# Moving weight splits, an exp table, four stores and a normalisation in a decoder layer

## The reference

```python
x = x + 0.5 * swiglu(rms_norm(x, g_ffn1), w1_ffn1, w3_ffn1, w2_ffn1)      # width 2816
z = rms_norm(x, g_mix) @ w_in + b_in                                      # q | k | v | u | v_gate
attn_out, k_state, v_state = attend(q, k, v)         # window of 128, softmax with a sink per head
vg = layer_norm(gelu(vg), gm_ln_g, gm_ln_b)
gm_out = gelu(u) * chunk_spatial_mix(vg, gm_w_s, gm_b_s)
x = x + concat([attn_out, gm_out]) @ w_out + b_out
x = x + 0.5 * swiglu(rms_norm(x, g_ffn2), w1_ffn2, w3_ffn2, w2_ffn2)
x = x + sigmoid(rms_norm(x, g_ple) @ w_ple_gate) * (ple @ w_ple_proj)
y = rms_norm(x, g_final)
```

## Time and profile before

| | us |
|---|---|
| median of 3 runs | 942.0 |
| lowest, highest | 941.59, 943.26 |
| the profiled execution | 943.26 |
| its span in the trace | 941.5 |
| TensorE busy | 927.4 (98%) |
| VectorE busy | 747.5 (79%) |
| ScalarE busy | 584.9 (62%) |
| GpSimd busy | 231.4 (25%) |

### The profile page before, as it was taken

The page is one execution under the profiler, slowest core; times in us unless marked ns, Lnnn a source line. Parts: engine busy times, 40 slices in busy tenths (PEclk is TensorE's granted clock), DMA queues, the critical chain, the costliest instruction groups (busy, mean ns, idle before and its releaser), DMA issues.

```text
span 941.5 us, 19772 instructions
## 1 busy us (share of the span) xinstructions
PE 927.4 (98%) x7702; PEld 915.2 (97%) x7702; DVE 747.5 (79%) x1293; ACT 584.9 (62%) x973; POOL 231.4 (25%) x181
## 2 busy tenths in 40 slices
PE   7999999999999999999999999999999999999997
PEld 7999999999999999989999999999999999999897
DVE  6979977888888686667866588987788888869586
ACT  7748746666667574756544566775676676657343
POOL 0212222223222220000319412222222322222221
PEclk9999999999999999999999999999999999999999
DMA  8958888778887789221133798877777887778702
GB/s 249 179 102 169 152 170 160 143 141 160 170 160 140 136 162 219 69 68 46 52 96 91 140 174 162 171 151 151 164 148 133 174 171 137 160 165 172 142 24 92
DMA packets 253385, 133.42 MB, mean 142 GB/s; under 512 B 15594, under 2 KB 249412, under 8 KB 253276
## 3 DMA queue, kind: packets, MB, share of 16 engines
q1 hardware_dynamic: 177820, 93.55, 36.0%
q0 software_dynamic: 75136, 37.76, 32.4%
q10 hardware_dynamic: 336, 0.84, 0.3%
HBM read 129.57 MB, written 3.59 MB: 141 GB/s over the span
## 4 chain that ended last, share of the span: by engine, by line
PE 54%; issue 28%; POOL 9%; DMA 4%; DVE 3%; ACT 2%; SPq 1%; POOLq 0%; DVEq 0%; ACTq 0%
PE ps L2079 30%; PE ps L1990 18%; POOL w_lo L1264 4%; POOL w_lo L1272 4%; PE ps L2421 2%; PE ps L2024 1%; DMA w_lo<-in_w_in_dram 1%; PE ps L2108 1%; DMA w_lo<-in_w_ffn_dram 1%; DMA w_lo<-in_w_ple_gate_dram 1%; DMA x_rows<-in_x_prompt_dram 1%; PE ps L2297 1%; POOL w_lo L1236 1%; PE ps L2326 1%; DMA w_raw<-in_w_ffn_dram 1%
## 5 line engine op out<-in xcount | busy, mean ns | idle before, releaser
L2079 PE MATMUL ps<-xo_hi,w_lo 128*128 128x260 f32 x1008 | 284.8, 283 | 0.0
L2079 PE MATMUL ps<-xo_hi,w_hi 128*128 128x260 f32 x1008 | 284.4, 282 | 0.0
L2079 PE MATMUL ps<-xo_lo,w_hi 128*128 128x260 f32 x864 | 244.3, 283 | 0.0
L2079 PEld LDWEIGHTS ps<-xo_hi,w_hi 128*128 128x128 f32 x1008 | 189.9, 188 | 0.0
L2079 PEld LDWEIGHTS ps<-xo_hi,w_lo 128*128 128x128 f32 x1008 | 189.9, 188 | 0.0
L1500 DVE TENSOR_TENSOR w_lo<-w_raw,w_hi 128x512 fp32r<-128x512 f32 (+1 forms) x180 | 174.4, 983 | 14.3 <-ACT w_hi L941 7.2
L2079 PEld LDWEIGHTS ps<-xo_lo,w_hi 128*128 128x128 f32 x864 | 162.7, 188 | 0.0
L2079 PE MATMUL ps<-hop_hi,w_hi 128*128 128x260 f32 x560 | 158.6, 283 | 0.6 <-ACT snap L972 0.5
L2079 PE MATMUL ps<-hop_hi,w_lo 128*128 128x260 f32 x560 | 158.4, 283 | 0.0
L2079 PE MATMUL ps<-hop_lo,w_hi 128*128 128x260 f32 x560 | 158.1, 282 | 0.0
L1264 POOL DMA_DIRECT2D w_lo<-in_w_ffn_dram x60 | 76.8, 1279 | 276.4 <-ACT w_lo L948 276.4
(11 more groups left out here) (320 smaller groups left out, 2058.8 us busy)
## 6 DMA issues: line engine op xcount, KB each, us to landing
w_raw<-in_w_ffn_dram SPq DMA_DIRECT2D x88, 256.0 KB, 4.4
w_lo<-in_w_ffn_dram POOLq DMA_DIRECT2D x88, 256.0 KB, 5.5
w_a<-in_w_ffn_dram SPq DMA_DIRECT2D x36, 512.0 KB, 5.8
w_raw<-in_w_ffn_dram SPq DMA_DIRECT2D x20, 512.0 KB, 5.9
w_a<-in_w_ffn_dram SPq DMA_DIRECT2D x32, 192.0 KB, 4.0
w_raw<-in_w_ffn_dram SPq DMA_DIRECT2D x32, 192.0 KB, 4.1
w_lo<-in_w_ffn_dram POOLq DMA_DIRECT2D x32, 192.0 KB, 5.1
w_raw<-in_w_in_dram SPq DMA_DIRECT2D x10, 512.0 KB, 4.7
```

The source lines that it names most:

```text
L2079: ins = pe.matmul(ps[:, b, 0:Q], w[:, cc, k * P:(k + 1) * P], m_, start=(first and k == 0 and t == 0), stop=(k == kn - 1 and t == 2), skip ...
```

## The change

- In `ffn_steps()` the steps `("hi","next",3)` and `("hi","next",4)` go. In the first stage their splits move into the mixer, to steps (1,2) and (2,2), by a wider condition in ACT's and POOL's loops. In the second stage ACT and POOL do keys 3, 4 and 5 of the last stage (gates 1, 2, 3) right behind `ffn_stage(1)`, where key 5 stood alone.
- Tables: units 3, 5 and 7 of the mixer move from DVE's subtraction to `summed`; gates 1, 2 and 3 move from `summed` to POOL's subtraction. DVE's remaining subtractions for units 4 and 13 come at other steps.
- `stat_spread` and `evac` 0 and 1 move from step (2,1) to (2,0).
- The five `norm` steps move from (11,7) to (12,0); `norm_rsqrt` stays.
- The exp on one column is removed.
- The four window stores are issued by ACT behind the copies of `kv_turn`, behind a wait for them, no longer by SP.

```diff
@@ ffn_steps
-                steps += [("lo", "next", 2), ("hi", "next", 3), ("hi", "next", 4)]
+                steps.append(("lo", "next", 2))
@@ mixer_steps
-        (2, 1): [("stat_spread",), ("evac", 0), ("evac", 1)],
+        (2, 0): [("stat_spread",), ("evac", 0), ("evac", 1)],
-        (11, 7): [("s_take",), ("norm_rsqrt",), ("norm", 3), ("norm", 4), ("norm", 0), ("norm", 1), ("norm", 2)],
+        (11, 7): [("s_take",), ("norm_rsqrt",)],
+        (12, 0): [("norm", 3), ("norm", 4), ("norm", 0), ("norm", 1), ("norm", 2)],
@@ hybrid_decoder_layer
-        summed = [("up", 0, n) for n in range(4, N_STD)] + last_keys(0)[:2]
-        summed += [("up", 1, n) for n in range(3, N_STD)] + last_keys(1)[:2] + last_keys(1)[3:6]
-        first_out = [("in", u) for u in range(3, 8)] + [("in", u) for u in range(8, N_IN)] + [("out", m) for m in range(3)]
-        low_steps = [("gemm", 1, 6), ("gemm", 1, 7), ("gemm", 3, 7), ("gemm", 4, 7), ("gemm", 5, 7)] + [("gemm", u - 2, 7) for u in range(8, N_IN)] + [("gemm", 12, 7), ("gemm", 13, 2), ("out", 0, 4)]
+        summed = [("up", 0, n) for n in range(4, N_STD)] + last_keys(0)[:2] + last_keys(0)[3:8:2]
+        summed += [("up", 1, n) for n in range(3, N_STD)] + last_keys(1)[:2]
+        first_out = [("in", 4), ("in", 6)] + [("in", u) for u in range(8, N_IN)] + [("out", m) for m in range(3)]
+        low_steps = [("gemm", 2, 7), ("gemm", 4, 7)] + [("gemm", u - 2, 7) for u in range(8, N_IN - 1)] + [("gemm", 12, 0), ("gemm", 12, 7), ("gemm", 13, 2), ("out", 0, 4)]
@@ sync
-            def store_windows():
-                ... (four dma_start)
-                elif u == 8:
-                    store_windows()
@@ scalar and gpsimd, loop over the mixer's steps
-                if kind == "gemm" and arg[1] == (2 if arg[0] < 6 else 5) and 2 < arg[0] < 13:
+                if kind == "gemm" and arg[1] == (2 if arg[0] < 6 else 5) and 0 < arg[0] < 13:
@@ scalar
-                elif kind == "scores" and arg[0] == 0:
-                    nc.scalar.activation(s_st[:, 6:7], ones[0:64, 0:1], ACT.Exp)
                     nc.scalar.activation(k_rows[0:TS, 1, :], ps[0:TS, 7, 2 * P:3 * P], ACT.Copy).then_inc(kv_taken, 1)
+                    act.wait_ge(kv_taken, 4)
+                    act.dma_start(o["v_win_prompt"]...)
+                    ... (the other three, as they were on SP)
@@ scalar and gpsimd, behind ffn_stage(1)
-            split_hi(last_keys(1)[5])
+            for key in last_keys(1)[3:6]:
+                split_hi(key)
```

More of the change, by code:

```diff
@@ L1117, in _ @@
                     nc.scalar.activation(k_rows[0:TS, 1, :], ps[0:TS, 7, 2 * P:3 * P], ACT.Copy).then_inc(kv_taken, 1)
+                    act.wait_ge(kv_taken, 4)
+                    act.dma_start(o["v_win_prompt"][0, 0].rearrange("w h d -> w (h d)"), v_rows[:, NB - 1, :]
+                                  ).then_inc(out_done, 16)
+                    act.dma_start(o["k_win_prompt"][0, 0].rearrange("w h d -> w (h d)"), k_rows[:, 0, :]
+                                  ).then_inc(out_done, 16)
+                    act.dma_start(o["v_win_sample"][0, :, W - 1].rearrange("b h d -> b (h d)"), v_rows[0:TS, NB, :]
+                                  ).then_inc(out_done, 16)
+                    act.dma_start(o["k_win_sample"][0, :, W - 1].rearrange("b h d -> b (h d)"), k_rows[0:TS, 1, :]
+                                  ).then_inc(out_done, 16)
                 elif kind == "soft":
@@ L1319, in _ @@
             ffn_stage(1)
-            split_lo(last_keys(1)[5])
+            for key in last_keys(1)[3:6]:
+                split_lo(key)
             clear_ssq(4)
```

## The result

The changed kernel takes 949.9 us (median of 4 runs, 948.41 to 950.1) against 942.38 us for the kernel before beside it: the ratio is 1.0077, with a 95% interval of 1.0058 to 1.0094. It is 7.5 us slower. I had forecast 944.6 in a range up to 947.4: the direction was right, the size too small, and the time lies outside the range. Run again beside three other kernels it took 949.94 us against 941.39, a ratio of 1.0093 (1.0078 to 1.0108). A ratio in this text is estimated from all runs of the two kernels, not divided out of the medians; the two can differ by up to 0.13%.

What follows compares the result with a forecast made beforehand. PE, busy 98% of the span, was taken as the bound. From the profiled 943.26 us, -2.1 - 1.6 + 1.1 + 1.7 + 1.9 + 0.3 = +1.3 gave 944.5, from the median 944.9; forecast 944.6, range 941.2 to 947.4.

Steps and rivals of the forecast that it cites:

- Part 1: Last stage's gates 1 to 3 by GpSimd's subtraction: DMA wait -2.1, low-clock stretch -1.6, VectorE's held add +1.1 us.
- Part 2: First softmax: exp's table load and four store issues on ACT start the first exp 3.07 us later; PE stalls +1.7.
- Part 3: Mixer units 3, 5 and 7 summed by DMA: unit 3's lands 10.2 us after issue, +1.9 us; units 5 and 7 cost 0.
- rival B: At unit 3 the copies hold the DMA: 4.8 us instead of 1.9, plus low clock; 948.4 at most; chance 0.12.
- bound of 4.8: Upper case for PE's wait at unit 3: 3.3 us of delay added to 8.2, plus 1.6 of spread.
- bound of 3.5: Upper bound of PE's wait at unit 3 if its DMA lands 11.8 us behind issue.
- The clock: Rival: any new wait of 1.7 or 1.9 us brings a low-clock stretch there, +1.6 us, 946.2; chance 0.16.
- Part 4: Norms at (12,0) end at about 462.6, +0.3 us, from -0.1 to +0.9; spread at (2,0) 0, up to +0.3.

Runs made afterwards that it cites:

- experiment 1: The changed kernel with unit 3 of the mixer back on VectorE's subtraction: 945.91 us, ratio 1.0041 to the kernel before.
- experiment 3: The kernel before with the one-column exp removed (941.85 us), the four window stores moved to ACT (941.34 us), or both (943.48 us).
- experiment 2: The changed kernel with the two 508 KB window copies issued behind the load of the mixer's last unit: 944.45 us, ratio 1.003.

## Why the prediction was wrong

- **Part 1 held.** The DMA wait of 2.1 and the stretch behind it went, and the add held by GpSimd cost 0.95 where I had 1.1. The kernel with the gates alone and the one with the wait show both halves. The forecast's -2.1, -1.6 and +1.1 are -2.1, -1.6 and +0.95 in the profiles. By the medians the gates alone won 1.8 us, not 2.75; it would fit if only some executions of the kernel before have the stretch, which isn't shown.
- **Part 2 held.** +1.7 forecast, 1.6 measured, alone (1.61) as in the changed kernel (1.62), and each edit alone inside the slack or 0.3 over (I had both inside). The drain of the Trainium skill, "ScalarE: Activation LUTs", section "What `ACT_TABLE_LOAD` costs", would have made it 3.1. What I did not see is that the issues on ACT need not take what they took on SP: in two kernels they took 2.31 and 2.97 us instead of 1.66, and the wait was 2.3 and 2.9.
- **Part 3 failed, in size: "An accumulating DMA issued among them should get some of the same delay, so I place it in the slow half, at 10.2".** The copies do hold the DMA, the mechanism of rival B, but by 6.3 us (13.4 against 7.1 without them), not by 2: the wait was 5.2 instead of 1.9. My bound of 4.8 had taken the 3.3 us of delay that unit 5's load had shown and some spread on top, and was nearly enough; but I gave it 0.12 and ended the range below it. Before, that load was the only large transfer beside the two copies. Now there are two, and the load took 11.5 us itself, not 8.0. The value of 10.2 and the bound of 3.5 were taken from the distribution of the DMA's own kind (6.2 to 11.8), and none of those 16 had met such copies.
- **The clock.** I had given the low-clock stretch behind a new wait 0.12 and 0.16 of chance, and 1.6 us. It came, behind the 5.2 us, and cost 2.5. Behind the 1.6 us at the softmax none came. In the balance of the two profiles the wait and the clock at unit 3 are 7.7 us, as much as the whole result; taking them away won only 2.7 to 3.7 (experiment 1), since the softmax's wait and a stretch behind it grew in turn. Rival B's own sum was off as well: it names a stretch of 1.6 us and adds 0.9. With 1.6 it makes 949.1, near what was measured, and outside the range all the same.
- **Part 4 failed in one term: "end at about 462.6, +0.3".** The +0.3 at the spatial product was right (0.26). The +1.2 us at `mix_lo` was missing. I had named its cause ("POOL's output rows hold the port pair") as the upper bound of 0.9, and valued it at nothing in the sum. I had looked at the wait that the norms end in, not at the chain of VectorE behind it, which has no slack: PE had waited 0.17 us at its end already. The spread at (2,0) cost nothing, as forecast.

In terms of the sum: 944.5 forecast; +3.3 for unit 3's wait, +2.5 for its clock, +1.2 for `mix_lo`, -0.4 for the wait at unit 0, -0.2 for parts 1 and 2 make 950.9, where the profiled execution took 950.45.

## What to carry to other kernels

Before a DMA is put on a tight path, list every transfer that will be in flight with it, and above all large DRAM-to-DRAM copies: measured landing times of its kind hold only for the company that they were measured in. Where a GpSimd operation and a VectorE operation meet on operands in SBUF, one of the two pays: VectorE where GpSimd had begun (2.52 us for an add of 0.69), GpSimd where VectorE was at work without a gap (2.90 us for 8 columns). So when anything shifts either stream, look for the new meetings along the whole chain, and where there is slack, let GpSimd wait for VectorE's last such operation (one wait was worth some 0.9 us here). Slacks are not additive: two edits of 1.3 and 1.7 us at one slack of 1.3 cost 0 and 0.3 alone and 1.6 together.

## What the runs showed of the hardware

- A low-clock stretch doesn't follow a wait of some length each time. The waits at gate 1 of 2.38 and 2.11 us in two kernels of experiment 3 have, over 885 to 890, the rows (exp removed, then stores moved):

```profile
885.00:890.00 5.00, 3.75 (x21) 3.78 (x22) 2.16 (x13) 0.00 (x0) 2.11 (x2) 0.73 1.11 197
```
```profile
885.00:890.00 5.00, 3.65 (x30) 3.68 (x31) 2.47 (x15) 0.00 (x0) 2.11 (x2) 1.00 1.19 208
```

  The first had a low-clock stretch, the second none, while the kernel before had one behind 2.07 us; so between 2.07 and 2.11 it isn't the length of the wait that decides. At the softmax none came behind 2.28 us (experiment 2) and one behind 2.93 (experiment 1).

  The 12 runs with both edits fall into two groups, 941.63 to 941.84 (5) and 943.42 to 944.09 (7), 2.0 us apart in the mean, a little more than the size of this stretch. The mean granted clock of the first group's runs is 0.999 to 1.0, that of the second's 0.996 to 0.999. It fits a stretch that comes in some executions of one kernel and not in others; as only the profiled ones show where the clock fell, it isn't shown.
- The four stores' issues on ACT held up the first exp by 1.66 us in the changed kernel and by 2.31 and 2.97 us in experiments 2 and 1 (the table load's [2.31 <-issue] and [2.97 <-issue]), with single issues of up to 1.04 us instead of 0.46. There unit 5's summing DMA had been issued 1.9 and 2.6 us ahead of the first store, in the changed kernel 4.1, and in experiment 3, where the issues took 1.65 us, there is none. That the one comes from the other wasn't tried.
- How the two copies hold a DMA issued ahead of them, whether by the size of their packets or by the engines that they take, stays open; shown is only that they do.
